# Windowed attention in a long float32 kernel: bias made ahead of the values' low parts, four gates on GpSimd, two blocks' halves before the last tile

## What is computed

```python
def odd_mixer(h, w_in, sink, w_out, slopes):
    proj = h @ w_in
    qc, kc, vc, gc = jnp.split(proj, [C_Q, C_Q + C_KV, C_Q + 2 * C_KV], axis=-1)
    oc = windowed_sink_attention(qc, kc, vc, sink, slopes)
    return (oc * jax.nn.silu(gc)) @ w_out
...
    sc = einsum(qb, kb) * scale + bias
    m = maximum(max(sc), sink)
    p = exp(sc - m)
    denom = sum(p) + exp(sink - m)
    o = einsum(p / denom, vb)
...
    x = x + gate[:, None, :] * y
return rms_norm(x, final_norm)
```

## Time and profile before

| | |
|---|---|
| median of 3 runs | 3027.79 us (3027.22 to 3028.67) |
| the profiled execution | 3027.36 us, span 3025.5 us, mean granted TensorE clock 0.984 |
| TensorE matmul (PE) | 2891.0 us, 96% of the span, 14578 instructions |
| weight load (PEld) | 2413.6 us, 80%, beside matmuls |
| VectorE (DVE) | 1731.7 us, 57% |
| ScalarE (ACT) | 1243.9 us, 41% |
| GpSimd (POOL) | 423.2 us, 14% |
| DMA | 219.28 MB, mean 72 GB/s |

### The profile page before, as it was taken

How to read it: one execution, slowest core, us unless ns; L and a number is a source line. 1 busy time by engine, 2 the same in 40 slices (tenths; PEclk the granted TensorE clock), 3 DMA queues, 4 the chain that set the end, 5 groups by cost and what they waited for, 6 DMA issues and landing times.

```text
span 3025.5 us, 37063 instructions
## 1 busy us (share of the span) xinstructions
PE 2891.0 (96%) x14578; PEld 2413.6 (80%) x14578; DVE 1731.7 (57%) x2258; ACT 1243.9 (41%) x2028; POOL 423.2 (14%) x352
## 2 busy tenths in 40 slices
PE   8999998899999999999999999998999899999998
PEld 6877886687888888888888777787888787888976
DVE  6564476663554444444444745688888835317874
ACT  5221456332443111111112335577767724427851
POOL 0000005200000000000000000255544300004520
PEclk9999999999999999999999999999999999999999
DMA  4111334032222233322331222100001212131031
GB/s 145 56 42 50 126 105 184 26 118 84 91 63 72 73 91 98 92 81 75 87 93 42 76 88 63 56 1 5 15 15 39 98 59 88 49 91 57 22 112 70
DMA packets 226587, 219.28 MB, mean 72 GB/s; under 512 B 9456, under 2 KB 195056, under 8 KB 224880
## 3 DMA queue, kind: packets, MB, share of 16 engines
q1 hardware_dynamic: 214752, 174.90, 18.5%
q0 software_dynamic: 6912, 25.17, 2.8%
q10 hardware_dynamic: 4752, 16.84, 1.5%
HBM read 180.12 MB, written 34.67 MB: 71 GB/s over the span
## 4 chain that ended last, share of the span: by engine, by line
PE 86%; DVE 7%; ACT 3%; issue 2%; POOL 2%; DMA 0%; SPq 0%; ACTq 0%; DVEq 0%; POOLq 0%
PE P L342 61%; PE P L280 5%; PE P L2409 3%; PE P L311 2%; POOL T L2669 2%; PE P L283 1%; PE P L285 1%; PE P L284 1%; PE P L2423 1%; PE P L1104 1%; PE P L2422 1%; DVE PTL L1517 1%; DVE WST L2648 1%; PE P L3010 1%; PE P L1552 1%
## 5 line engine op out<-in xcount | busy, mean ns | idle before, releaser
L267 DVE TENSOR_TENSOR wl<-wf,wh 128x1024 fp32r<-128x1024 f32 (+4 forms) x239 | 251.6, 1053 | 923.8 <-ACT wh L259 923.5
L259 ACT ACTIVATE wh<-wf 128x1024 fp32r<-128x1024 f32 (+4 forms) x239 | 219.8, 920 | 1030.1 <-PE P L342 985.6
L342 PE MATMUL P<-AQ,wh 128*128 128x512 f32 x1824 | 489.4, 390 | 5.8 <-issue 3.0
L342 PE MATMUL P<-XH,wh 128*128 128x512 f32 (+1 forms) x1264 | 396.1, 395 | 8.9 <-DVE XL L1346 5.2
L342 PEld LDWEIGHTS P<-AQ,wh 128*128 128x128 f32 x1824 | 341.3, 188 | 77.9 <-issue 4.6
L342 PE MATMUL P<-XL,wh 128*128 128x512 f32 (+1 forms) x1264 | 391.2, 391 | 0.0
L342 PE MATMUL P<-XH,wl 128*128 128x512 f32 (+1 forms) x1264 | 391.2, 391 | 0.0
L2669 POOL TENSOR_TENSOR T<-T,WST 128x1024 f32<-128x1024 f32 x128 | 242.6, 1895 | 573.8 <-DVE WST L2641 573.8
L342 PEld LDWEIGHTS P<-XH,wh 128*128 128x128 f32 (+1 forms) x1264 | 235.7, 187 | 65.5 <-issue 14.6
L342 PE MATMUL P<-AQ,wl 128*128 128x512 f32 x912 | 280.8, 389 | 0.0
L342 PEld LDWEIGHTS P<-XL,wh 128*128 128x128 f32 (+1 forms) x1264 | 236.2, 187 | 52.6
(11 more groups left out here) (438 smaller groups left out, 5006.2 us busy)
## 6 DMA issues: line engine op xcount, KB each, us to landing
AW<-ada_w POOLq DMA_DIRECT2D x48, 512.0 KB, 4.1
wf<-w_gate_up SPq DMA_DIRECT2D x44, 512.0 KB, 3.8
H<-scratch_h SPq DMA_DIRECT2D x32, 512.0 KB, 6.5
wf<-w_in SPq DMA_DIRECT2D x28, 512.0 KB, 3.8
scratch_h<-H SPq DMA_DIRECT2D x24, 512.0 KB, 5.7
scratch_g<-T ACTq DMA_DIRECT2D x22, 512.0 KB, 3.0
wf<-odd_w_in SPq DMA_DIRECT2D x20, 512.0 KB, 3.8
wf<-even_w_in SPq DMA_DIRECT2D x17, 512.0 KB, 3.8
```

The source lines that it names most:

```text
L259: e.activation(self.sb["wh"][i % 2][:, 0:m], self.sb["wf"][i % 2][:, 0:m], ACT.Copy).then_inc(*self.s.w_hi.up(i))
L267: e.tensor_tensor(l, f, h.bitcast(F32), ALU.subtract).then_inc(*self.s.w_lo.up(i))
L342: ins = e.matmul(self.P[slot][0:m, t:t1], w, x[:, k, t:t1], start=first and k == 0, stop=last and k == kb - 1)
```

## The change

VectorE makes the bias of head pair 0 ahead of the four low parts of the values (the function is moved out as `dve_bias`), and TensorE no longer waits for the last of these ahead of the scores. GpSimd multiplies O2[j] with the gate for j = 0 to 3, behind the scaling of tiles 20, 28, 36 and 44. ScalarE makes XH[0] and XH[1] in steps 40 and 44, behind the exponentials of tiles 39 and 43; VectorE makes XL[0] and XL[1] in step 67, ahead of the last output sum. Behind that, VectorE does gates 4 to 7, each ahead of the low half of block j - 2. SyncE loads four blocks of H, gate blocks 4 and 5, four blocks of H, gate blocks 6 and 7.

```diff
@@ dve_odd
         self.dve_tiles(e, "go", lambda e, j: None)
+        self.dve_bias(e, 0, 0)
+        self.dve_bias(e, 0, 1)
         for j in range(2):
             for i in range(2):
                 self.dve_low(e, ("V2", j, i), sb["V2"][j][:, 4 * i:4 * i + 4, :, 64:128], self.v2_source(j, i),
@@ sp_windowed
         e.wait_ge(*s.mm.to(("ws", 63)))
-        self.sp_reload(e, "back3")
-        for j in range(4, 8):
-            e.wait_ge(*s.lo.to(("oo", j - 4)))
-            e.dma_start(self.T[j % 4], self.dr["gT"][:, j, :]).then_inc(*s.gl[j].up("end"))
+        for h in range(2):
+            self.sp_reload(e, "back3", range(4 * h, 4 * h + 4))
+            for j in range(4 + 2 * h, 6 + 2 * h):
+                e.wait_ge(*s.lo.to(("oo", j - 4)))
+                e.dma_start(self.T[j % 4], self.dr["gT"][:, j, :]).then_inc(*s.gl[j].up("end"))
@@ pe_windowed
-        e.wait_ge(*s.lo.to(("V2", 1, 1)))
         e.wait_ge(*s.dve.to(("k2l", 3)))
@@ act_windowed
+            if n in (40, 44):
+
+                j = (n - 40) // 4
+                e.wait_ge(*s.mm.to(("wv", 31)))
+                e.wait_ge(*s.pool.to(("o2", j)))
+                e.activation(self.XH[:, j, :], self.T[j], ACT.Copy).then_inc(*s.hi.up(("oo", j)))
             at = n - 4
@@ dve_windowed
-        bias(0, 0)
-        bias(0, 1)
         for n in range(69):
+            if n == 67:
+
+                for j in range(2):
+                    self.dve_low(e, ("oo", j), self.XL[:, j, :], self.T[j], self.XH[:, j, :])
             at = n - 2
@@ pool_windowed
             if n < 56 and n % 8 == 2:
                 sink(n // 8 + 1)
+            if n in (20, 28, 36, 44):
+                j = (n - 20) // 8
+                e.wait_ge(*s.gl[j].to("end"))
+                e.wait_ge(*s.dve.to(("wo", 4 * j + 3)))
+                e.tensor_tensor(self.T[j], self.sb["O2"][j][:, :], self.T[j], ALU.mult).then_inc(*s.pool.up(("o2", j)))
@@ act_odd_out
-        for j in range(8):
-            e.wait_ge(*s.dve.to(("o2", j)))
+        e.wait_ge(*s.mm.to(("wv", 63)))
+        for j in range(2, 8):
+            e.wait_ge(*(s.pool if j < 4 else s.dve).to(("o2", j)))
             e.activation(self.XH[:, j, :], self.T[j % 4], ACT.Copy).then_inc(*s.hi.up(("oo", j)))
@@ dve_odd_out
-        gate(0)
-        for j in range(8):
-            if j < 7:
-                gate(j + 1)
+        for j in range(2, 8):
+            if j < 6:
+                gate(j + 2)
             self.dve_low(e, ("oo", j), self.XL[:, j, :], T[j % 4], self.XH[:, j, :])
```

More of the change, by code:

```diff
@@ L836, in sp_spill, with sp_reload @@
             e.dma_start(self.dr["hT"][:, j, :], self.H[:, j, :]).then_inc(*self.s.h[j].up(name))
-    def sp_reload(self, e, name):
-        for j in range(8):
+    def sp_reload(self, e, name, blocks=range(8)):
+        for j in blocks:
             e.dma_start(self.H[:, j, :], self.dr["hT"][:, j, :]).then_inc(*self.s.h[j].up(name))
@@ L3072, in act_windowed, with dve_bias @@
                 e.activation(self.w_lower(p), self.w_out(p)[64:128, :], ACT.Copy).then_inc(*s.act.up(("lower", p)))
+    def dve_bias(self, e, hp, q):
+        s = self.s
+        f, h, l = (self.sb[name][hp % 2][:, q, :] for name in ("BF", "BH", "BL"))
+        e.wait_ge(*s.pool.to(("sink", hp)))
+        e.tensor_copy(h, f).then_inc(*s.dve.up(("bias high", hp, q)))
+        e.wait_ge(*s.dve.here())
+        if q == 0:
+            e.tensor_tensor(l, f, h.bitcast(F32), ALU.subtract).then_inc(*s.dve.up(("bias", hp, 0)))
+        else:
+            for c in (0, 386):
+                e.tensor_tensor(l[:, c:c + 2], f[:, c:c + 2], h[:, c:c + 2].bitcast(F32),
+                                ALU.subtract).then_inc(*s.dve.up(("bias", hp, 1) if c else None))
     def dve_windowed(self, e):
         s, sb = self.s, self.sb
[L3077 to L3088, removed]
-        bias(0, 0)
-        bias(0, 1)
         for n in range(69):
+            if n == 67:
+                for j in range(2):
+                    self.dve_low(e, ("oo", j), self.XL[:, j, :], self.T[j], self.XH[:, j, :])
             at = n - 2
@@ L3117, in dve_windowed @@
             if n < 56 and n % 8 in (5, 6):
-                bias(n // 8 + 1, n % 8 - 5)
+                self.dve_bias(e, n // 8 + 1, n % 8 - 5)
     def pool_windowed(self, e):
```

## The result

The changed kernel takes **3034.91 us** (median of 11 runs, 3032.53 to 3037.62) beside 3027.79 us for the kernel before in the same session (11 runs, 3025.40 to 3028.67): ratio 1.0026, 95% interval 1.0017 to 1.0034. It is 7.1 us slower, and the forecast was 3024.9 us. The profiled execution is the slowest of the 11: 3037.62 us, span 3035.8 us, mean granted clock 0.982. Its span is 10.2 us over that of before, 3.1 us more than the medians differ, since it is the slowest of its 11 and has the lowest mean clock of them (the others have 0.983 or 0.984).

What follows compares the result with a forecast made beforehand. The kernel was taken as bound by TensorE (96% of the span). Terms -1.7 + 2.8 + 0.65 - 4.6 = -2.85 us on the profiled 3027.36, on the median's scale 3024.9 us; range 3020.8 to 3029.8.

Steps and rivals of the forecast that it cites:

- Start, -1.7: Ahead of the attention's first scores: bias before the low parts starts the scores 1.7 us earlier, between 1.3 and 2.6.
- a clock that stays up: At the first scores: if the clock does not fall, the start gains 2.6 us instead of 1.7.
- Four gates, +2.8: In the attention: each GpSimd gate exceeds 1.68 us of idle time by 0.7 us, four times, 2.8 us later.
- the nearest rows' price: At each gate: 2.37 us for a GpSimd multiplication of two full tensors, less 1.68 us idle, costs 0.7 us.
- the rival: At the gates: VectorE's next bias cast waits for the gate's end, 1.56 us each, 6.2 in all; chance 0.3.
- ScalarE's copies, +0.65: After the exponentials of tiles 39 and 43: two copies cost 0.1 and 0.55 us, together 0.65, between 0.2 and 1.3.
- End, -4.6: First output pair: output matmuls start without a wait and the pair ends 4.6 us earlier, bounds 1.6 and 6.7.
- The wait at block 2: In the output pair: TensorE waits 1.0 us because gate 4 precedes low part 2 on VectorE.
- The wait at block 4: In the output pair: block 6's load stands behind four H blocks, so TensorE waits 2.0 us more.
- the fall to half clock goes too: In the output pair: the fall, about 2.3 us, vanishes since no wait is above 2 us; included in the -4.6.
- held cast and late loads at once: Gates and end together, with dearer copies: over 3033.9 us, slower by more than about 0.2%; chance 0.03.

Runs made afterwards that it cites:

- the first part alone: Kernel before, with only the bias of head pair 0 moved ahead of the low parts and TensorE's wait taken off the scores: 3023.53 us, ratio 0.9989.
- half gates: Changed kernel with each of GpSimd's four gates split into two operations of 128x512, the second three tiles later: 3025.28 us, ratio 0.9994.
- the maximum: Changed kernel with VectorE rounding the bias by a two-input max(f, f) in place of the cast, gates unmoved: 3035.71 us, ratio 1.0027.

## Why the prediction was wrong, step by step

- **Start, -1.7: right.** The gap shrank by 1.71 us. The clock fell at the new start, as forecast, but stayed down for 3.3 us of work and not 5.3. Of the up to 0.9 us that the forecast named for a clock that stays up, this shorter stretch gave 0.5, in the run with the first part alone and, by the sum below, in the changed kernel.
- **Four gates, +2.8: the step that failed.** It read "I take 0.7, as it is the nearest rows' price, with the other beside it as a rival". The 0.7 is the price of a gate whose length alone counts; the run with the cast moved away measured 0.7 over the kernel before, and 1.0 over its own head pairs without a gate. With the cast beside it, the rival held: it had forecast 1.56 us a gate. The fourth head pair, with no fall of the clock, is longer by 1.59, of which 0.2 is ScalarE's second copy, so a held gate costs 1.4. "No row shows a VectorE operation lengthened beside GpSimd" was the weak argument: the same paragraph had said that the two never meet in the trace of before, so its silence was no evidence.
- **Missing from all cases: the clock behind the new gaps.** The first three of the four head pairs last 1.26 to 1.39 us more than the fourth (24.35, 24.30 and 24.22 against 22.96), as TensorE ran 3.2 us at 1.2 GHz behind the gap; with the second copy, which only the fourth has, taken off it, a fall costs 1.5 to 1.6, half of the 3.2. The middle is then four holds of 1.4, falls of 4.6 in all and a copy of 0.2, less the 0.5 from the start: +9.9, and not the rival's +6.9 (6.2 and the copies). The forecast had asked of the clock only at the two gaps that the change removes, and not at the four it might make.
- **ScalarE's copies, +0.65: too dear.** The first, forecast at 0.1, costs nothing (24.22 beside 24.35; with the cast moved 22.11 beside 22.11). The second, forecast at 0.55, costs 0.2 (with the cast moved 22.32, with half gates 21.86 beside 21.62).
- **End, -4.6: the mechanism was right, a size was off, and it tipped the clock.** The wait at block 2 was forecast at 1.0 us and is 1.00, in part by luck: the shortest landing of the four loads is 4.3 us and not 3.6, and the first two blocks end 0.7 us later than forecast, so that both ends of the wait moved alike. The wait at block 4 was forecast at 2.0, with block 6 landing in the time that a queue of 419 GB/s needs for what is ahead of it; it is 3.60. The statement "the fall to half clock goes too, since no wait is above 2 us" fell with it: 5.7 us of work at 1.2 GHz are 2.85 us lost. These two terms (1.6 and 2.85) and the 0.49 us at the first matmul are 4.9 of the 5.5 us that the end missed; the other 0.6 is not assigned. The 0.49 was in the forecast's own numbers: it has the low half of block 0 done at 2912.6 and lets TensorE, which waits for both halves, start on it at 2912.2. That the four H blocks are the cause of the long wait is shown by the loads put first. Its size is that of one execution: with the same order of loads, the wait at block 4 is 2.70, 2.73, 2.23 and 3.37 us with the gates later, the cast moved, the maximum and the half gates, and the pair ends 28.07, 28.19, 26.36 and 27.42 us after the last values. So the forecast's 2.0 is below all five.
- **Range and chances.** The measured 3034.9 lies outside 3020.8 to 3029.8. The case "held cast and late loads at once" had 0.03 for slower by over 0.2%; it is what came, with the falls of the clock on top.

What stays open: which gaps bring the clock down. Gaps alike in length went both ways: 1.55 to 1.58 us three times down and once not, in the changed kernel and again with the loads first; 1.75 us once down in four; at the end 2.70, 2.73 and 3.60 us down, but 2.23 and, in the run with half gates, 3.37 us not. The windows behind the 2.70 us (gates later) and behind the 3.37 us:

```profile
2925.90:2928.80 2.90, 2.81 (x7) 2.23 (x8) 2.90 (x4) 1.06 (x1) 0.00 (x0) 0.50 0.58 144
...
2928.20:2932.00 3.80, 3.76 (x17) 3.11 (x17) 3.80 (x4) 1.06 (x1) 0.00 (x0) 1.00 0.32 83
```

The cost is measured, the condition is not.

## What to carry to other kernels

Before work is put on GpSimd next to VectorE, list what VectorE has queued in that stretch: here a cast from SBUF to SBUF and an operation with two SBUF inputs waited out the whole GpSimd operation (1.72 and 1.92 us for 0.35 and 0.55), and everything queued behind them waited along. The cure is cheap, another place for the long operation or a shorter one. A trace in which two things never meet says nothing of what they do when they meet. And each new wait of TensorE is to be priced twice, with the clock up and with some 1.3 to 2.9 us for a fall behind it.

## What was not expected of the hardware

- A fall of TensorE's clock behind a gap of only 1.55 us, which is followed by transposes: 3.2 us at 1.2 GHz, and 1.5 to 1.6 us lost.
- A two-input VectorE operation of 388 values is held by a GpSimd operation as the cast is (1.92 us for 0.55), while a maximum over PSUM runs beside it unchanged at 0.95 us.
- The held operation's row has its start before the gate's end and its length stretched. There is no idle time in front of it, so the list of waits doesn't show it; the mean of its group does (745 ns for 352).
